# Gate tiles 32 to 79 of the input projection in the pair form, with halves added on GpSimd and one sigmoid for four tiles

## What is computed

```python
proj = h @ w_in[l]
hq, hf, hi, hg, su, sq, sk, sv, gates = jnp.split(proj, split_at, axis=-1)
o_a = hgrn2_mixer(...); o_b = s5_mixer(...); o_c = stick_breaking_mixer(...)
gate = jax.nn.sigmoid(gates)
merged = (gate[..., :D_MODEL] * (o_a @ w_branch[l, 0])
          + gate[..., D_MODEL:2 * D_MODEL] * (o_b @ w_branch[l, 1])
          + gate[..., 2 * D_MODEL:] * (o_c @ w_branch[l, 2]))
x = x + merged @ w_out[l]
hf2 = rms_norm(x, norm_ffn_g[l])
up = causal_depthwise_conv(hf2 @ w_up[l], conv_w[l])
x = x + (jax.nn.silu(up[..., :D_FF]) * up[..., D_FF:]) @ w_down[l]
```

## Time and profile before

| | us |
|---|---|
| median of 3 runs | 1393.51 |
| lowest and highest of the 3 | 1393.4, 1394.25 |
| the profiled execution | 1393.05 |
| its span | 1391.5 |

### The profile page before, as it was taken

One profiled execution on the slowest core, in us unless ns is written; L12 is line 12 of the kernel. 1 busy time (PEld: TensorE's weight loads), 2 busy tenths in 40 slices (PEclk: granted clock), 3 DMA queues, 4 the chain that ended last, 5 costly groups with the idle time before them and its releaser, 6 DMA issues.

```text
span 1391.5 us, 27921 instructions
## 1 busy us (share of the span) xinstructions
PE 1387.0 (100%) x9886; PEld 1280.6 (92%) x9886; DVE 1034.2 (74%) x1427; ACT 755.1 (54%) x1056; POOL 143.2 (10%) x187
## 2 busy tenths in 40 slices
PE   9999999999999999999999999999999999999999
PEld 8999999999999999988888888888888888888888
DVE  7999857899889678776687777777777775455453
ACT  7575676754544554545655555555555554444432
POOL 1200000000000024322111111111111110000000
PEclk9999999999999999999999999999999999999999
DMA  8655545446564656766566555655656656666663
GB/s 287 187 185 180 181 156 179 145 162 198 171 195 161 196 182 218 222 188 193 174 202 193 192 187 182 193 194 185 188 189 194 182 178 198 207 188 201 195 202 111
DMA packets 76513, 261.70 MB, mean 188 GB/s; under 512 B 8800, under 2 KB 10368, under 8 KB 76448
## 3 DMA queue, kind: packets, MB, share of 16 engines
q1 hardware_dynamic: 74304, 255.89, 57.8%
q0 software_dynamic: 1424, 4.37, 1.1%
q10 hardware_dynamic: 720, 0.53, 0.1%
HBM read 258.66 MB, written 2.10 MB: 187 GB/s over the span
## 4 chain that ended last, share of the span: by engine, by line
PE 98%; ACT 1%; DMA 1%; DVE 0%; SPq 0%; issue 0%; ACTq 0%
PE bank L376 40%; PE bank L390 28%; PE bank L378 21%; PE bank L416 5%; PE pair L435 1%; PE bank L401 1%; DMA x_first<-xT 0%; DMA raw<-w_in 0%; PE pair L572 0%; ACT w_hi L743 0%; ACT gates L753 0%; PE pair L441 0%; SPq L298 0%; PE pair L543 0%; ACT L753 0%
## 5 line engine op out<-in xcount | busy, mean ns | idle before, releaser
L1076 DVE TENSOR_TENSOR w_lo<-raw,w_hi 128x1024 fp32r<-128x1024 f32 x496 | 584.8, 1189 | 292.9 <-ACT w_hi L743 288.2
L743 ACT ACTIVATE w_hi<-raw 128x1024 fp32r<-128x1024 f32 x496 | 508.7, 1030 | 411.4 <-PE bank L378 198.5
L376 PE MATMUL bank<-h,w_hi 128*128 128x512 f32 x1408 | 488.4, 390 | 0.0
L378 PE MATMUL bank<-h,w_lo 128*128 128x256 f32 x1408 | 397.1, 282 | 0.0
L390 PE MATMUL bank<-a_in,w_hi 128*128 128x256 f32 x2048 | 362.1, 280 | 0.0
L376 PEld LDWEIGHTS bank<-h,w_hi 128*128 128x128 f32 x1408 | 264.4, 188 | 55.4
L390 PEld LDWEIGHTS bank<-a_in,w_hi 128*128 128x128 f32 x2048 | 311.8, 188 | 3.1 <-issue 2.1
L390 PE MATMUL bank<-a_in,w_lo 128*128 128x256 f32 x1024 | 285.6, 279 | 0.0
L378 PEld LDWEIGHTS bank<-h,w_lo 128*128 128x128 f32 x1408 | 266.1, 189 | 0.0
L376 PE MATMUL bank<-act,w_hi 128*128 128x512 f32 x660 | 228.8, 390 | 0.0
L390 PEld LDWEIGHTS bank<-a_in,w_lo 128*128 128x128 f32 x1024 | 192.5, 188 | 0.0
(11 more groups left out here) (234 smaller groups left out, 1364.4 us busy)
## 6 DMA issues: line engine op xcount, KB each, us to landing
raw<-w_up SPq DMA_DIRECT2D x176, 512.0 KB, 3.7
raw<-w_in SPq DMA_DIRECT2D x156, 512.0 KB, 4.3
raw<-w_down SPq DMA_DIRECT2D x80, 512.0 KB, 4.4
raw<-w_out SPq DMA_DIRECT2D x32, 512.0 KB, 4.2
raw<-w_br SPq DMA_DIRECT2D x16, 512.0 KB, 3.6
raw<-w_br SPq DMA_DIRECT2D x16, 256.0 KB, 3.3
raw<-w_down SPq DMA_DIRECT2D x16, 256.0 KB, 2.7
x_first<-xT SPq DMA_DIRECT2D x8, 256.0 KB, 5.7
```

What stands on the lines that cost most here:

```text
L376: pe.matmul(bank[b][:, :], w[:, k * P:(k + 1) * P], a.rearrange("p a t -> p (a t)"), start=first and n == 0, stop=False, skip_group_check= ...
L378: mm = pe.matmul(bank[b][:, 0:SEQ], l[:, k * P:(k + 1) * P], a[:, 0, :], start=False, stop=last and n == len(blocks) - 1, skip_group_check ...
L743: act_e.activation(w_hi[s][:, 0:blocks * P], raw[s][:, 0:blocks * P], ACT.Copy).then_inc(hi_ready, 1)
L1076: ve.tensor_tensor(w_lo[s][:, w], raw[s][:, w], w_hi[s][:, w].bitcast(F32), ALU.subtract).then_inc(lo_ready, 1)
```

## The change

From tile 32 on the input projection's tiles are in the pair form. ScalarE copies the right half of the bank into half (Copy) and the left half into gates (Copy). GpSimd adds the two in gates (48 adds of 128x256). ScalarE then takes the sigmoid of four tiles in one instruction (128x1024), in place, twelve times: for g = 0 to 10 at the end of out_tile(37), out_tile(41) and so on to out_tile(77), and for the last four after the first GLU gate. New waits: ScalarE's copy to half waits for the add two tiles before, the sigmoid waits for its four adds, the GLU's first copy waits for all 48 adds, and VectorE's first product with a gate waits for all 12 sigmoids.

```diff
+PAIR_T = 32
@@ TensorE
-                    in_piece(n, h, a_raw if n < NORM_T else a_in).then_inc(piece_used, 1)
+                    if n < PAIR_T:
+                        mm = in_piece(n, h, a_raw if n < NORM_T else a_in)
+                    else:
+                        mm = piece(n % BANKS, 2 * n + h, 2 * n + h, range(PIECE), lambda k: a_in[:, PIECE * h + k, :, :], h == 0, h == 1)
+                    mm.then_inc(piece_used, 1)
@@ ScalarE, out_tile(n)
+                if n >= PAIR_T:
+                    i = n - PAIR_T
+                    if i >= 2:
+                        act_e.wait_ge(S("gate_summed"), i - 1)
+                    act_e.activation(half[i % 2][:, :], bank[n % BANKS][:, SEQ:2 * SEQ], ACT.Copy).then_inc(S("gate_half"), 1)
+                    act_e.activation(proj(n), bank[n % BANKS][:, 0:SEQ], ACT.Copy).then_inc(tile_out, 1)
+                    if i > 4 and i % 4 == 1:
+                        gate_sigmoids(i // 4 - 1)
+                    return
                 act_e.activation(proj(n), bank[n % BANKS][:, 0:SEQ], ACT.Sigmoid if n >= 8 * CT else ACT.Copy).then_inc(tile_out, 1)
+
+            def gate_sigmoids(g):
+
+                act_e.wait_ge(S("gate_summed"), 4 * g + 4)
+                j = PAIR_T + 4 * g - 8 * CT
+                act_e.activation(gates[:, j:j + 4, :], gates[:, j:j + 4, :], ACT.Sigmoid).then_inc(S("gate_sig"), 1)
@@ ScalarE, GLU
+            act_e.wait_ge(S("gate_summed"), IN_TILES - PAIR_T)
             for m in range(CT):
@@
                 glu_gate(m)
+                if m == 0:
+                    gate_sigmoids((IN_TILES - PAIR_T) // 4 - 1)
@@ VectorE, ahead of the branches
             ve.wait_ge(tile_out, IN_TILES - NORM_T)
+            ve.wait_ge(S("gate_sig"), (IN_TILES - PAIR_T) // 4)
@@ GpSimd
+            for n in range(PAIR_T, IN_TILES):
+                i = n - PAIR_T
+                pool.wait_ge(S("gate_half"), i + 1)
+                pool.wait_ge(tile_out, n - NORM_T + 1)
+                pool.tensor_tensor(proj(n), proj(n), half[i % 2][:, :], ALU.add).then_inc(S("gate_summed"), 1)
```

## The result

| | before | changed |
|---|---|---|
| median us (runs) | 1393.54 (6) | 1400.57 (6) |
| lowest, highest | 1393.4, 1394.42 | 1400.22, 1401.2 |
| profiled execution, span | 1393.05, 1391.5 | 1400.66, 1399.1 |

The ratio is 1.0049, with a 95% interval of 1.0039 to 1.0059. The forecast was 1393.4, with a range of 1391.6 to 1396.0.

A forecast was written before the change was run, and what follows sets the result against it. Between tiles 32 and 79 the number and spacing of TensorE's matmuls alone were taken to set the end. -2.72 + 2.56 + 0.1 = -0.06 us on the profiled 1393.05 gave a median of 1393.4 us, range 1391.6 to 1396.0.

The forecast's parts named there:

- TensorE's gain: Tiles 32 to 79: pair tiles 5.547 us apart instead of 5.600, a gain of 2.72 us in all.
- The sigmoid at tile 37: ScalarE at tile 37: a Sigmoid table load and four-tile sigmoid make the chain behind it 2.05 us late.
- Two adds on the chain: Adds of tiles 38 and 39 hold VectorE 0.36 us each before lo(82); stall at tile 41 2.56 us.
- The 0.60 of hold: A GpSimd add meeting busy VectorE keeps its next instruction with two SBUF operands from starting, up to 0.60 us.
- What that wait sets off: Behind tile 41's stall of 2.56 us: TensorE itself late, granted clock 1.0 throughout, no further loss there.
- Tight places: Slack of a piece's lo before TensorE's first matmul: 0.46 us at tile 41, 1.46 at 50, 2.50 at 58.
- the next tight pieces keep their distance: Behind tile 41: lo(84) at most 2.7 us late, TensorE's tile 42 1.5, against a little over 2 of slack.
- The S5 stretch: Tiles 50, 58, 66 and 74: adds against slack cost 0.1 us for all together, ends 0 and 1.0.
- Rival D: VectorE becomes the bound in the S5 stretch: 2.5 to 3.5 us of stalls, 1396 to 1397; chance 0.11.
- The prediction's own sign of being wrong: Wrong if tile 41 starts on time, or PE waits for w_lo in S5 over a microsecond in all.

The follow-up runs named there:

- e3: Changed kernel with its first three four-tile sigmoids all at tile 45 and every GpSimd add cut to one column; 1391.58 us, ratio 0.9984.
- e5: Changed kernel with one-column GpSimd adds from tile 45 on, full adds for tiles 32 to 44; 1397.62 us, ratio 1.0030.
- e2: Changed kernel with every GpSimd add cut to one column of 256, sigmoids in place; 1393.84 us, ratio 0.9999.
- e1: Changed kernel with its first three four-tile sigmoids all at tile 45, full adds; 1400.48 us, ratio 1.0043.
- e9: Changed kernel with the pair form from tile 48 only, VectorE adding the halves (left from PSUM) instead of GpSimd, first four-tile sigmoid at tile 53; 1392.11 us, ratio 0.9989.
- e4: Kernel before (plain form, single sigmoids) with 48 spare GpSimd adds of 128x256, results unused; 1398.30 us, ratio 1.0032.
- e8: Changed kernel with VectorE adding the halves instead of GpSimd, one ScalarE copy less a tile, three sigmoids at tile 45; 1396.10 us, ratio 1.0016.
- e7: Changed kernel with GpSimd adds of 128 of the 256 columns at all 48 tiles; 1395.33 us, ratio 1.0012.
- e6: Changed kernel with one-column GpSimd adds for tiles 32 to 44, full adds from 45 on; 1396.75 us, ratio 1.0020.
- e10: Changed kernel with one-column GpSimd adds and two write-only 128x256 GpSimd fills behind each; 1393.60 us, ratio 0.9999.

## Why the prediction was wrong, step by step

**TensorE's gain: right.** 5.545 a tile were measured, and the stage of e3 is 2.11 us shorter with 0.56 of waits left in it, 2.7 in all.

**The sigmoid at tile 37: right.** ScalarE of the changed kernel, from the copies of tile 37 on (timeline; here ScalarE's hi is L748):

```profile
239.49 0.36 ACT L780 ACTIVATE half<-bank 128x256 f32<-128x256 f32 x1
239.75 0.37 ACT L781 ACTIVATE gates<-bank 128x256 f32<-128x256 f32 x1
240.14 1.28 ACT L791 ACT_TABLE_LOAD   x1
241.44 1.06 ACT L791 ACTIVATE gates<-gates 128x1024 f32<-128x1024 f32 x1
242.40 1.49 ACT L867 ACTIVATE tmp<-pair 128x768 f32<-128x768 f32 x2
243.99 1.49 ACT L758 ACTIVATE tmp<-tmp 128x1536 f32<-128x1536 f32 x1
...
251.63 1.49 ACT L758 ACTIVATE tmp<-tmp 128x1536 f32<-128x1536 f32 x1
```

Tile 37's first copy is at 239.49, 1.64 later than the old 237.85, and Abs at 243.99, 3.64 later than 240.35: the chain lost 2.00 us, 2.05 were forecast. (The 1.64 are the later start of the whole profile, 0.8, and the wait at tile 35, less 0.1 for faster tiles.) The load is followed by the sigmoid 0.02 us after its end, so the drain that ScalarE: Activation LUTs in the Trainium skill ("What ACT_TABLE_LOAD costs") adds to a switch doesn't show here.

**Two adds on the chain: right, a little short.** VectorE and GpSimd behind the Ln:

```profile
253.15 3.97 DVE L1130 SCALAR_TENSOR_TENSOR tmp<-tmp 128x1536 f32<-128x1536 f32 x2 [1.31 <-ACT tmp L758]
257.16 2.23 DVE L1123 TENSOR_TENSOR tmp<-tmp,upper 128x256 f32<-128x256 f32 x4
259.42 2.36 DVE L1099 TENSOR_TENSOR w_lo<-raw,w_hi 128x1024 fp32r<-128x1024 f32 x2
```

```profile
253.95 1.55 POOL L1728 TENSOR_TENSOR gates<-gates,half 128x256 f32<-128x256 f32 x1 [11.79 <-ACT gates L781]
256.39 1.34 POOL L1728 TENSOR_TENSOR gates<-gates,half 128x256 f32<-128x256 f32 x1 [0.89 <-ACT gates L781]
```

The two long instructions took 3.97 instead of 3.55 and the masks 2.23 instead of 1.80: 0.85 us, 0.72 were forecast. Tile 41 lost 2.74, 2.56 were forecast. The 0.60 of hold behind this leaves L1588 0.42 us of work where its row says 0.48 alone; with 0.48 the hold is 0.54, and the most that an add made an instruction of this stage longer is 0.57.

**What that wait sets off: missed.** The windows of PE (us, busy and count, granted clock, DMA share, GB/s):

```profile
256.00:261.00 5.00, 2.42 (x15) 1.00 0.01 2
261.00:264.00 3.00, 3.00 (x13) 0.69 0.75 214
264.00:266.00 2.00, 2.00 (x9) 0.61 0.54 203
266.00:270.00 4.00, 4.00 (x26) 1.00 0.51 154
```

Three steps inside tile 41, in its timeline:

```profile
260.79 0.47 PE L377 MATMUL bank<-a_in,w_hi 128*128 128x512 f32 x1 [2.58 <-DVE w_lo L1099]
...
261.21 0.40 PE L377 MATMUL bank<-a_in,w_hi 128*128 128x512 f32 x1
...
263.00 0.63 PE L377 MATMUL bank<-a_in,w_hi 128*128 128x512 f32 x1
...
263.63 0.63 PE L377 MATMUL bank<-a_in,w_hi 128*128 128x512 f32 x1
```

After the wait of 2.58 us the steps first kept their 0.35; from 262.2 to 265.5 they are 0.64 apart, at the lower of the two levels, 1.2 GHz. This takes 1.63 us of TensorE, although it is shown busy. The prediction took a wait at its own length.

But here it is hardly a cause of the loss, since TensorE meets the next wait all the earlier without it. e5 lost less to the clock in tile 41 and more at sb_o: 1.39 + 1.28 = 2.67 us, the changed kernel 1.63 + 0.99 = 2.62. And of the six runs of the changed kernel two have a mean granted clock of 1.000 and took 1400.22 and 1400.53 us, three have 0.999 and took 1400.49 to 1400.66, and one has 0.998 and took 1401.2. A mean that rounds to 1.000 leaves room for 1.4 us at the lower level at most (an estimate, 0.0005 x 1399 / 0.5), less than half of the 3.3 seen here.

**"Tight places": the reading that failed.** I had looked for slack only where a piece's lo is needed, and put "the next tight pieces keep their distance" behind tile 41. Two small products in PE's order were as tight, and none had a wait before, so that the waits view didn't name them. VectorE and TensorE of the kernel before:

```profile
223.59 1.02 DVE L1107 SCALAR_TENSOR_TENSOR norm_rows<-tmp,second_row,softp_lo 128x768 fp32r<-128x768 f32 x1
...
281.27 0.68 DVE L1408 TENSOR_TENSOR proj<-pair,gates 128x512 f32<-128x512 f32 x1
```

```profile
224.88 0.51 PE L517 MATMUL pair<-norm_rows,two_rows 32*128 32x256 f32 x8
...
282.10 0.67 PE L435 MATMUL pair<-tmp,proj 128*128 128x256 f32 x2
```

norm_rows ended at 224.61 and its product began at 224.88; L1408 gave the pair of banks back at 281.95 and sb_o, which needs it, began at 282.10. With 0.27 and 0.15 us of room the first paid 1.23 us and the second 0.99. For norm_rows the changed kernel's timeline of VectorE shows how (0.95 before became 1.49, and the tensor_scalar's 0.69, with a single input from SBUF, became 1.11); another 0.2 us are a lo that begins later behind ScalarE's copies, and 0.2 TensorE's faster tiles:

```profile
217.36 1.49 DVE L1123 TENSOR_TENSOR tmp<-tmp 128x768 f32<-128x768 f32 x1
...
222.13 1.11 DVE L1126 TENSOR_SCALAR gates<-gates 128x1024 f32<-128x1024 f32 x1
```

At sb_o it isn't the last instruction that is held. VectorE ends L1431 5.76 us later than before, measured from tile 32's first matmul, and tile 45 begins 5.76 later. Of these 2.86 were there when the Ln released VectorE (0.96 from the wait at tile 35, 2.00 from the sigmoid, 0.1 back for faster tiles), and 2.90 were added on the way to sb_o, by the adds: e2 has none of them. The prediction followed these holds for two instructions and four masks, up to lo(82), and no further.

**The S5 stretch: the term that was mis-sized.** I took 0.1 us for tiles 50, 58, 66 and 74, with 1.0 as the upper end; it was 2.6 (0.21, 1.17, 0.83, 0.36). An add cost less than the 0.60 I had put on it, but there were more of them than I counted. I counted the four adds of tiles 54 to 57 against the slack at tile 58. But VectorE's run ahead of that lo is longer. It begins with the two lo of tile 49, after the last wait for ScalarE of over a microsecond, in both kernels, and ends with lo(116):

```profile
310.15 2.36 DVE L1099 TENSOR_TENSOR w_lo<-raw,w_hi 128x1024 fp32r<-128x1024 f32 x2 [1.34 <-ACT w_hi L748]
...
365.87 2.35 DVE L1099 TENSOR_TENSOR w_lo<-raw,w_hi 128x1024 fp32r<-128x1024 f32 x2
```

From 310.15 to 365.87 + 1.22 = 367.09 are 56.9 us; before it was 303.44 to 357.41, 54.0 us, with 1.8 us of pauses, of which 0.4 are left. Ten adds fall on it and cost VectorE 3.0 + 1.4 = 4.4 us together, 0.44 each. 1.4 of this went into the pauses; of the other 3.0, and of 0.5 us by which TensorE had caught up with the run, 2.5 were slack, and tile 58 lost the rest, 1.17 with the start-up behind the wait. Rival D said just this ("one more add in the way") and priced it at 2.5 to 3.5 us; it was the S5 part of the truth, and had 0.11. No rival joined it with waits elsewhere. The prediction's own sign of being wrong is there too: PE waits for w_lo in the S5 stretch for 1.9 us, more than the microsecond it allowed.

**In the sum:** -2.7 as forecast; tile 41 2.7 against 2.6; 1.6 of clock, 1.2 and 1.0 at the two products, against nothing; 2.6 against 0.1 in S5; and 0.3 in small amounts. That is 6.8 for a forecast of about zero. Up to tile 45 the sum can be told by VectorE alone, without the clock: 5.8 us late there, and then the S5 stretch. The forecast was no change; measured were 7.0 us, 0.5%.

## What to carry to other kernels

A helper engine that reads SBUF takes its time from VectorE, and where VectorE is nine tenths busy count the instructions that fall on its whole unbroken run, not those of the last few tiles before the deadline. Read the slack of every consumer in the bound engine's order, the small products and the buffers they need back included, since a waits view without lines says only that nobody waits yet. And when a wait is cured, look at who is late next before counting the gain, and at what the cure itself puts in the way: e1 removed 2.6 us of wait and won nothing, while e9 left the tight stretch alone and kept 1.6.

## What the hardware showed that I had not expected

In the profiled executions TensorE's granted clock fell to its lower level after waits of 2.58 us (the changed kernel), 2.57 (e5) and 2.46 (e1, at sb_o), and stayed at 1.0 after 1.73 (e2), 1.8 (e4), 2.0 (e8) and 2.02 (e7). About 2 us isn't safe, though: five of e7's ten executions and seven of e8's have a mean of 0.999 (no profile shows where), while all 36 of e2, e4, e6 and e10, with a longest wait of 1.7 to 1.8, have 1.000. What a fall costs depends on what comes behind it. In e7, as in the changed kernel, it costs next to nothing (a median of 1395.34 us with 0.999 and 1395.15 with 1.000). In e8 it costs about 1.5 us (1395.59 to 1397.13 against 1394.01 to 1395.23), and in e1, with one run at 1.000, about 1.7 (1400.47 to 1400.85 against 1398.79); there the long wait is at sb_o, the last tight place of the stick-breaking stretch. In the changed kernel it was low from 1.4 us behind the first matmul after the wait, for about 3.3 us; in e5 that first matmul was slow already, and by 263.5, 2.9 us later, the clock was back (1.39 us lost). In e1's windows it is seen at sb_o (us, PE busy and count, granted clock, DMA share, GB/s):

```profile
282.00:285.00 3.00, 1.18 (x8) 1.00 0.60 175
285.00:288.00 3.00, 2.36 (x10) 0.79 0.50 178
288.00:291.00 3.00, 3.00 (x13) 0.64 0.50 162
291.00:294.00 3.00, 3.00 (x19) 1.00 0.59 187
```

GpSimd waits as well, even for almost nothing: e10's add of one column took 0.19 us at best and 0.62 in the median, and up to 1.25, the length of a lo. It isn't let in between any two instructions of VectorE either: in the changed kernel an add that began at 333.66 took 2.52 us and ended 0.60 behind the second of two lo that ran from 333.22 to 335.58, at their usual 1.22 each.
